# Hybrid decoder block: gate quarters over 110 expert tiles, first block ranked in the queries, picks in halves

## The reference, cut to what matters

```python
# x: 1024 tokens x 1024; mixers (retention, short convolution) come first
def peer_ffn(a, w_q, k1, k2, u, v):                 # a = rms_norm(h)
    q = (af @ w_q).reshape(t, PEER_HEADS, 2, PEER_HALF)              # 8 heads, 2 x 128
    s1 = jnp.einsum('thd,hnd->thn', q[:, :, 0], k1)                  # 128 keys a side
    s2 = jnp.einsum('thd,hnd->thn', q[:, :, 1], k2)
    v1, i1 = lax.top_k(s1, PEER_TOPK); v2, i2 = lax.top_k(s2, PEER_TOPK)      # 16
    cand_s = v1[..., :, None] + v2[..., None, :]                     # 16 x 16 per head
    top_s, top_pos = lax.top_k(cand_s, PEER_TOPK)
    gate = jax.nn.softmax(top_s, axis=-1)            # 8 x 16 experts of 16384 per token
    act = jax.nn.gelu(jnp.einsum('td,ted->te', xb, ue))              # ue = u[idx]
    return jnp.einsum('te,ted->td', gb * act, ve)                    # ve = v[idx]
# then per-layer embeddings, gate and a last rms_norm
```

## Time and profile before

| | us |
|---|---|
| median of 3 runs (3942.32 to 3951.86) | 3949.08 |
| the profiled execution | 3940.36 |
| its span, first to last instruction | 3938.3 |
| PE busy, share of the span | 3514.5 (89%) |
| DVE busy | 2827.3 (72%) |
| POOL busy | 2409.5 (61%) |
| ACT busy | 1008.0 (26%) |
| expert stage, 128 tiles | 1548.1 to 2672.4 |
| value stage, 32 groups | 2672.4 to about 3775 |

### The profile page before, as it was taken

One profiled execution on the slowest core, in us unless ns is written; L12 is line 12 of the kernel. 1 busy time (PEld: TensorE's weight loads), 2 busy tenths in 40 slices (PEclk: granted clock), 3 DMA queues, 4 the chain that ended last, 5 costly groups with the idle time before them and its releaser, 6 DMA issues.

```text
span 3938.3 us, 59196 instructions
## 1 busy us (share of the span) xinstructions
PE 3514.5 (89%) x22379; PEld 3412.9 (87%) x22379; DVE 2827.3 (72%) x4151; ACT 1008.0 (26%) x1654; POOL 2409.5 (61%) x1612
## 2 busy tenths in 40 slices
PE   7899888878989889999999999997889989988877
PEld 6799788777989889988989899997888888888765
DVE  5524477866555654999999999635888888878854
ACT  2310221121000121144545455302222222212132
POOL 5488563325678776876766668865555555555522
PEclk9999899888999999999999999998999999999988
DMA  4244421114666767877878777877888888888811
GB/s 143 77 123 123 128 87 56 45 39 146 217 223 235 249 224 265 297 277 273 285 274 307 277 288 277 314 259 247 277 285 287 282 282 284 287 269 283 276 38 59
DMA packets 324293, 852.82 MB, mean 217 GB/s; under 512 B 27552, under 2 KB 125344, under 8 KB 320672
## 3 DMA queue, kind: packets, MB, share of 16 engines
q0 software_dynamic: 110592, 402.70, 28.0%
q1 hardware_dynamic: 72864, 258.15, 21.6%
q10 hardware_dynamic: 140672, 189.82, 13.8%
HBM read 755.67 MB, written 94.90 MB: 216 GB/s over the span
## 4 chain that ended last, share of the span: by engine, by line
PE 37%; DVE 12%; DMA 5%; POOL 3%; issue 3%; ACT 2%; ACTq 1%; DVEq 0%; POOLq 0%; SPq 0%
PE main L630 26%; PE main L869 7%; DVE h L1853 5%; DMA rows<-v_rows,s_idx 5%; DVE scr L1529 4%; PE scr L828 4%; POOL v_lo L595 2%; ACTq L1207 1%; ACT v_hi L1217 1%; DVE rows L1522 1%; DVE res L1864 1%; POOL rows L568 1%; POOL w_lo L541 0%; PE scr L728 0%; DVE hot L1787 0%
## 5 line engine op out<-in xcount | busy, mean ns | idle before, releaser
L541 POOL TENSOR_TENSOR w_lo<-raw,w_hi 128x1024 fp32r<-128x1024 f32 x346 | 873.2, 2524 | 27.9
L539 POOL CAST w_hi<-raw 128x1024 fp32r<-128x1024 f32 x346 | 367.8, 1063 | 677.5 <-issue 428.6
L630 PE MATMUL main<-mix_hi,w_hi 128*128 128x320 f32 (+1 forms) x2816 | 691.1, 320 | 84.1 <-POOL w_lo L541 44.1
L630 PE MATMUL main<-mix_lo,w_hi 128*128 128x320 f32 (+1 forms) x2816 | 677.9, 315 | 0.0
L630 PE MATMUL main<-mix_hi,w_lo 128*128 128x320 f32 (+1 forms) x2816 | 676.9, 315 | 0.0
L1529 DVE SCALAR_TENSOR_TENSOR scr<-rows,s_dot,scr 128x1024 f32<-128x1024 f32 x381 | 489.1, 1284 | 230.8 <-DMA rows<-v_rows,s_idx 219.0
L869 PE MATMUL main<-h_hi,v_hi 128*128 128x320 f32 x2048 | 490.5, 322 | 120.4 <-DVE res L1864 101.8
L630 PEld LDWEIGHTS main<-mix_hi,w_hi 128*128 128x128 f32 x2816 | 480.7, 191 | 91.5 <-issue 61.6
L568 POOL DMA_INDIRECT rows<-u_rows,s_idx x384 | 405.4, 1056 | 238.1 <-DVE s_dot L1522 134.2
L595 POOL TENSOR_TENSOR v_lo<-raw,v_hi 128x1024 fp32r<-128x1024 f32 x128 | 308.0, 2407 | 389.3 <-ACT v_hi L1217 378.1
L630 PE MATMUL main<-a_hi,w_hi 128*128 128x320 f32 (+1 forms) x1728 | 477.4, 331 | 70.3 <-POOL w_lo L541 43.8
(11 more groups left out here) (231 smaller groups left out, 4967.1 us busy)
## 6 DMA issues: line engine op xcount, KB each, us to landing
raw<-stream SPq DMA_DIRECT2D x474, 512.0 KB
act_d<-actb ACTq DMA_DIRECT2D x128, 320.0 KB
gate_d<-gbuf ACTq DMA_DIRECT2D x20, 2048.0 KB
h<-act_d ACTq DMA_DIRECT2D x128, 320.0 KB, 4.9
gate_in<-gate_d ACTq DMA_DIRECT2D x31, 1280.0 KB, 13.4
rows<-u_rows,s_idx POOLq DMA_INDIRECT x384
rows<-v_rows,s_idx POOLq DMA_INDIRECT x384, 5.8
score_d<-stage ACTq DMA_DIRECT2D x16, 320.0 KB
```

What stands on the lines that cost most here:

```text
L539: pool.tensor_copy(w_hi[:, s, :], raw[:, s, :]).then_inc(hi_made, 1)
L541: pool.tensor_tensor(w_lo[:, s, :], raw[:, s, :], w_hi[:, s, :].bitcast(F32), ALU.subtract) \
L630: last = pe.matmul(main[s][:, dst:dst + n], wt[:, s, c * P:(c + 1) * P], rows[:, c, src:src + n], start=(c == 0 and wt is w_hi and rows is ...
```

## The change

`LEAD` becomes 4 and `SPAN` 22, so that five blocks fill tiles 4 to 113. The 16 quarters of a block come behind tiles 1, 2, 3, 4, 6, 7, 8, 10, 11, 12, 14, 15, 16, 18, 19, 20 of its 22 (`QUARTERS`). The ranks of block 0 move into the queries (`rank_first`), on the scores as they lie in `stage`; before it overwrites `stage`, ACT waits until the last head's have been read. Each pick works in two halves of 4 heads (`pick_keys`): the first behind the rank of head 4, in the middle of the block, the second and the softmax (`pick_rest`) at its end. From the last block on `due` gives 3 rows a tile, so that 499 rows in place of 485 are done by the end of the expert stage, and 269 in place of 283 are spread evenly over the 31 groups. `rank` and the sparse ranks are written as generators, with the same order of instructions ahead of the queries.

```diff
-LEAD = 16
-SPAN = 18
+LEAD = 4
+SPAN = 22
+QUARTERS = [1 + q * (SPAN - 1) // 16 for q in range(16)]
...
-    return max(0, 5 * (min(tile, LAST_ROWS) - PICKED_AT) // 2)
+    steady = 2 * S1 + LEAD + SPAN * (ND - 1)
+    tile = min(tile, LAST_ROWS)
+    return max(0, 5 * (min(tile, steady) - PICKED_AT) // 2 + 3 * max(0, tile - steady))
...
+                if s == 0 and not (isinstance(h, int) and h == 0):
+                    act.wait_ge(head_ranked, h)
                 act.copy(stage[:, s, :], scr[1][:, 0:TDN]).then_inc(scr_drained[1], 1)
...
-                    if k == SPAN - 1 and j + 1 < ND:
+                    if k == QUARTERS[15] and j + 1 < ND:
                         softmax(NS + j + 1, sel_v)
                         if j + 2 < ND:
                             load_scores(j + 2)
...
             for tile in range(2 * Q_PAIR, 2 * S1):
                 dve.wait_ge(tile_done, 2 * S1 + tile)
                 dot_until(due(tile - 1))
+                h, odd = divmod(tile - 2 * Q_PAIR - 3, 2)
+                if h >= 0 and not odd:
+                    rank_first(h)
...
+            rank_first(PH - 1)
+            pick_begin(sel_v[:, :, :], gsum)
+            dot_until(due(2 * S1))
+            pick_keys(0)
+            dot_until(due(2 * S1 + 1))
+            pick_keys(1)
+            dot_until(due(2 * S1 + 2))
+            pick_rest(NS)
+            for j in range(ND):
+                if j + 1 < ND:
                     dve.wait_ge(score_in, 16 * j + 16)
                 for h in range(PH):
+                    if h == 0:
+                        dot_until(due(2 * S1 + LEAD + SPAN * j - 1))
+                        unpack(j)
+                    m = 16 * j + 2 * h
+                    for w in range(2):
+                        hots(m, w)
+                    dot_until(due(2 * S1 + tile_of(m) - 1))
+                    if j + 1 < ND:
+                        for _ in rank_dense(j + 1, h):
+                            pass
+                        if h == PH // 2:
+                            pick_keys(0)
+                        if h == PH - 1:
+                            pick_begin(sel_v[:, :, :], gsum)
+                    for w in range(2):
+                        hots(m + 1, w)
+                    dot_until(due(2 * S1 + tile_of(m + 1) - 1))
...
+                if j + 1 < ND:
+                    pick_keys(1)
+                    pick_rest(NS + j + 1)
...
-                    dot(2 if dt == DC - 1 else 1)
+                    dot(share(share(B_DOTS, b, NGRP - 1), dt, DC))
```

More of the change, by code:

```diff
@@ L96, in due, with share @@
 def due(tile):
-    return max(0, 5 * (min(tile, LAST_ROWS) - PICKED_AT) // 2)
+    steady = 2 * S1 + LEAD + SPAN * (ND - 1)
+    tile = min(tile, LAST_ROWS)
+    return max(0, 5 * (min(tile, steady) - PICKED_AT) // 2 + 3 * max(0, tile - steady))
 A_DOTS = due(LAST_ROWS)
+B_DOTS = DOTS - A_DOTS
+def share(total, i, n):
+    return total * (i + 1) // n - total * i // n
 RING = tuple(range(8))
@@ L597, in _ @@
                 if n >= EG:
-                    for _ in range(3 if n % EG == EG - 1 else 2):
-                        if at_row[0] < DOTS:
-                            gather()
+                    for _ in range(share(B_DOTS, n - EG, NE - EG)):
+                        gather()
             while at_row[0] < DOTS:
@@ L851, in _ @@
                         select(j)
-                    elif k <= 16:
-                        quarter(16 * j + k - 1, first=j if k == 1 else None)
+                    elif k in QUARTERS:
+                        quarter(16 * j + QUARTERS.index(k), first=j if k == 1 else None)
             with pe.Fori(0, (NE - LEAD - SPAN * ND) // 2) as i:
@@ L1160, in _ @@
                 act.wait_ge(score_st[s], 16 * PH + 16)
-            load_scores(0)
+            load_scores(1)
             def gelu(e):
@@ L1393, in settled, with rank @@
                 dve.wait_ge(dve_step, steps.n)
-            def rank(src, v, rest, pairs, pairs_left, index, value, between=lambda: None):
+            def rank(src, v, rest, pairs, pairs_left, index, value):
                 settled()
@@ L1399, in rank @@
                     steps.mark(dve.max(v[:, s, 0:8], src[s]))
-                between()
+                yield
                 settled()
@@ L1430, in rank_sparse, with sparse_parts @@
                 dve.wait_ge(sc_in, 2 * h + 2)
[L1431 to L1435, removed]
+                return rank((sc[:, t, 2 * h, :], sc[:, t, 2 * h + 1, :]), s_v16, s_left, s_cand, s_candl,
+                            lambda a, at: s_ix[:, t, h, a * TOPK + at:a * TOPK + at + 8],
+                            lambda at: s_top[:, t, h, at:at + 8])
+            def sparse_parts():
+                for n in range(NS * PH):
+                    yield from rank_sparse(n)
+                    yield
+            parts = sparse_parts()
             def rank_some(n):
                 for _ in range(n):
-                    if ranked[0] < NS * PH:
-                        rank_sparse(ranked[0])
-                        ranked[0] += 1
+                    next(parts, None)
             def pick_begin(values, sums):
@@ L1457, in pick_key @@
             def pick_key(ix, at, same, dst, which, between=lambda: None):
-                same4 = same[:, :, :].rearrange("p (h k) a -> p h k a", h=PH)
+                heads = ix.shape[1]
+                same4 = same[:, :, :].rearrange("p (h k) a -> p h k a", h=heads)
                 settled()
@@ L1468, in pick_key @@
                     same4, same4,
-                    ix[:, :, which * TOPK:(which + 1) * TOPK].unsqueeze(2).to_broadcast([P, PH, TOPK, TOPK]), ALU.mult))
+                    ix[:, :, which * TOPK:(which + 1) * TOPK].unsqueeze(2).to_broadcast([P, heads, TOPK, TOPK]), ALU.mult))
                 between()
@@ L1775, in _, with rank_first @@
             norm_rows(2, 1, 4 * DC, 0, a_lo[1], a_hi[1])
-            rank_some(6)
+            rank_some(48)
             mixers(1, lambda tile: dot_until(due(tile)))
+            def rank_first(h):
+                m = query_scratch(h, 1)
+                dve.wait_ge(scr_drained[1], m.drained("s1"))
+                for part, _ in enumerate(rank((stage[:, 0, 0:P], stage[:, 1, 0:P]), v16, left, cand, candl,
+                                              lambda a, at: sel_ix[:, h, a * TOPK + at:a * TOPK + at + 8],
+                                              lambda at: sel_v[:, h, at:at + 8])):
+                    if part == 2:
+                        settled()
+                        dve.sem_inc(head_ranked, 1)
             for tile in range(2 * Q_PAIR, 2 * S1):
@@ L1801, in rank_dense, with pick_keys, pick_rest @@
             def rank_dense(j, h):
[L1802 to L1812, removed]
+                return rank((scores[:, 2 * h, :], scores[:, 2 * h + 1, :]), v16, left, cand, candl,
+                            lambda a, at: sel_ix[:, h, a * TOPK + at:a * TOPK + at + 8],
+                            lambda at: sel_v[:, h, at:at + 8])
+            def pick_keys(half):
+                hs = slice(PH // 2 * half, PH // 2 * (half + 1))
+                ks = slice(P // 2 * half, P // 2 * (half + 1))
+                pick_places(sel_ix[:, hs, :], [at[:, hs, :] for at in pos])
+                for which in range(2):
+                    pick_key(sel_ix[:, hs, :], [at[:, hs, :] for at in pos], eq[:, ks, :], picked[:, :, ks], which)
+            def pick_rest(n):
+                pick_end(n, sel_v[:, :, :], gsum, picked[:, 2, :])
                 settled()
@@ L1819, in _ @@
             weigh_sparse(0)
-            for j in range(ND + 1):
-                if j < ND:
+            rank_first(PH - 1)
[8 more added lines that the diff above has]
+                if j + 1 < ND:
                     dve.wait_ge(score_in, 16 * j + 16)
                 for h in range(PH):
[L1824 to L1839, removed]
+                    if h == 0:
[15 more added lines that the diff above has]
+                    dot_until(due(2 * S1 + tile_of(m + 1) - 1))
+                if j == 2:
                     weigh_sparse(1)
-                if j < ND:
-                    pick(NS + j)
+                if j + 1 < ND:
+                    pick_keys(1)
+                    pick_rest(NS + j + 1)
             dot(A_DOTS - at_dot[0])
```

29 lines of the change are left out of this document (15 added, 14 removed).

## The result

The changed kernel takes 3986.36 us (median of 4 runs, 3978.29 to 3992.15), the kernel before 3947.32 beside it (4 runs, 3942.32 to 3951.86): ratio 1.0098, 95% interval 1.0075 to 1.012. It is 39 us slower; the forecast was 14 slower, and its range ended at 3983. The two profiled executions are 48 us apart (spans of 3938.3 and 3986.1), because the one before ran 7 us under its median.

A forecast was written before the change was run, and what follows sets the result against it. PE and DVE were taken as both nearly full, PE losing 79 us in the expert stage. Losses 49 + 23 + 14 + 12 = 98 against 79 (+19.1), value stage -5.4: 3949.1 + 13.7 = 3963, range 3920 to 3983.

The forecast's parts named there:

- (a): Middle of a block: the half pick delays quarter 9's `hots`; PE waits 10.5 and loses 1.7 to slow clock, 49 us.
- The dots that are missing meanwhile hurt nobody: Middle of a block: dots DVE doesn't make during the half pick cost nothing, since quarters wait first.
- (b): Block boundary: the score load queues behind `gate_d`, landing 15.5 after it; first quarters late, 7.8 at three boundaries, 23 us.
- my reason for the 33.6 us: Expert stage before the change: PE waits 33.6 us for `w_lo` because POOL's gathers wait for dots, not made during picks.
- rival 2: Boundary: the score load isn't late, or DVE arrives later anyway; 17 us less than the sum, 3946; chance 0.24.
- (c): Start of the expert stage: DVE's eighth rank, dots and pick make PE wait 11.5 at `select`; 14 us in all.
- (d): Small losses: quarter 15, 4 x 1.5; block 0's first quarters, 2.5; last block's dots and five gather buffers, 3; together 12.
- Rival 4: Last block: 3 rows a tile make the weight stream late, 1 us a tile over 16 tiles, 3979; chance 0.07.
- Rival 1: Expert stage: PE alone bounds it, DVE meeting its deadlines; about 50 us lost in place of 79, 3915; chance 0.22.
- The queries: Seven ranks add 38 us to DVE there, but it is busy only 47 of 128, so they cost nothing.
- DVE can't work ahead: Expert stage: `hots` can't be made before the last quarter is read, so what counts is where a long piece stands.
- The value stage: Even rows cost its groups 0; 2 dots in place of 6 before ACT's copy at the end give -5.4.

The follow-up runs named there:

- Experiment 4: The changed kernel with the half pick in the middle of a block moved behind the `hots` of quarter 9: 3954.68 us, ratio 1.0018.
- experiment 1: The changed kernel with PE's loop over the five blocks written out, nothing else: 3964.86 us, ratio 1.0047.
- experiment 3: The changed kernel with PE's block loop written out and DVE's wait for the scores moved ahead of the first rank: 3947.72 us, ratio 1.0001.
- experiment 6: The kernel before the change with only PE's loop over the blocks written out: 3951.38 us, ratio 1.0013.
- experiment 5: The changed kernel with the three edits: PE's block loop written out, score wait ahead of the first rank, half pick behind quarter 9's `hots`: 3921.76 us, ratio 0.9937.
- experiment 2: The changed kernel with DVE's wait for the next scores moved from ahead of `unpack` to ahead of the first rank reading them: 3977.52 us, ratio 1.0079.
- experiment 9: Third half of the `hots` buffer, added to the changed kernel with the three edits, LEAD 6 and 2.5 rows a tile: 3893.73 us, ratio 0.9867.
- experiment 7: The changed kernel with the three edits and LEAD 6 in place of 4: 3916.79 us, ratio 0.9932.
- experiment 12: The kernel before the change with only its value-stage rows spread evenly over the 31 groups: 3942.65 us, ratio 0.9989.

## Why the forecast had the sign right and the size wrong

- **(a), the middle: right.** 12.2 a block were forecast and 11.6 to 12.9 measured, at quarter 9, by the half pick ahead of its `hots`. Experiment 4 gives 32 of the 49 back by the place alone. "The dots that are missing meanwhile hurt nobody" held in the middle. The mechanism is the forecast's.
- **(b), the boundary: here the forecast failed.** The late load is there, and somewhat later than forecast: it lands 17 behind its issue (15.5), and DVE waits for it 23.6 us in three times, where I had some 5 each. But I took the time at which PE would be ready for the select as its tiles' sum, 7.04 each. The step that failed is this floor of PE at a boundary: PE's jump costs 4.2 to 5.0 us and about 2 of slow clock behind it, four times, a term that the sum doesn't have. The boundaries lost 41.7 in place of 23, and the fourth 7.8 where I had nothing. The sum was short by 18.7 there, out of 24. The trace of before had the four stops. One is printed as "issue", 3.9 us, which I passed over; three are printed as `w_lo`, and I took them for it, so that my reason for the 33.6 us (POOL's gathers wait for dots) is wrong for 13.1 of them. Experiments 1, 3 and 6 show that the stop goes with the loop, and that the old pick covered it; the instruction packets show what it is. The Trainium skill, "Runtime: NRT & Kernel Launch", section "Instruction fetch mechanics", says that a taken branch to code outside the window held near the engine must wait for its fetch, and recommends unrolling where possible. The trace agrees: a packet of the instruction queue in each stop, 4.2 to 5.0 us for a body of 22 tiles in the changed kernel, 3.9 to 4.7 for one of 18 in the kernel before; the loops over two tiles in the lead and the tail show no wait for "issue".
- **(b), rival 2** said that timely scores would give 17 back; taken off the boundary alone they gave 9, since PE's jump lay beside them. Term and rival had the same fault.
- **(c), the start:** 18.2 for 16.5. The wait at select was 10.70 (11.5 forecast). Tile 3 lost 5.4 by a late `w_lo`, for which I had 0.7; in experiments 1, 4 and 5 it lost 0.6, in experiment 2 again 5.4, so it varies. That the sums agree so nearly is in part luck.
- **(d):** quarter 15 as forecast. The last block's 3 was too little: the five buffers, which I priced at almost nothing, stall one tile by 6.8. Rival 4 had the place, and named the weight stream in place of the row buffers.
- **Rival 1** (PE alone is the bound) was the better design's forecast, not this one's: with the jumps gone, the places put right and a third half of `hot`, the kernel comes to 3885, beyond its 3915, while the sum of DVE's work is nearly the same.
- **The queries:** right, no new wait of PE. The sentence that "DVE can't work ahead", since `hots` cannot be made before the last quarter is read, was true of this kernel, and worth 17 us (experiment 9), of which 9 show in its expert stage.
- **The value stage:** the end as forecast (5.4; 5.9 measured). Its groups are open. By the profile the stage ended 1102.9 us behind tile 127 before and 1102.7 after, so its groups took back what the end gave. But in the six other profiles with the changed kernel's 269 rows (experiments 1 to 5 and 7) it took 1091.7 to 1105.4, and why experiment 1's was 8 shorter I can't say. The kernel before and experiment 6 have the same value stage, and there it took 1102.9 and 1112.1; so one profile each doesn't tell even 9 us of groups from chance. For the same reason the profile of experiment 12 (1108.5) doesn't show whether its end's 5.9 reach the whole time, and its median only just does.

## What to carry to other kernels

Count the jumps of every engine's loops among its work: price the first instruction behind each with a large body from the trace, also where another wait lies over it, for it stays when that wait goes. A wait's printed cause may be a neighbour that ended at about the same time: check which tile the named instruction belongs to. Where two engines are nearly full, cost a long piece by what waits behind it at its place, and look for the place where the consumer has its longest pause; moving one half pick gave 32 us here, more than the 23 by which the three edits together beat the kernel before. And when two late things meet at one place, try the edits together as well as apart: alone these two showed 18 of the 29 us that they take off the boundaries.

## What I had not expected of the hardware

A jump back over PE's code of 22 tiles costs 4.2 to 5.0 us in the changed kernel and 3.6 to 4.9 in experiments 2 and 4, one over 18 tiles 3.9 to 4.7, while jumps over two tiles don't show. In all 16 of these stops a 16 KB packet of the instruction queue starts 1.0 to 2.4 us after PE's last matmul, and PE starts again 1.6 to 1.8 us behind its end. The 16 DMA engines are fully busy there (share 0.99 to 1.01 in the changed kernel's four), about four fifths of it with what ACT's queue moves; whether the fetch would be shorter without them isn't tested. Behind the changed kernel's four stops PE ran at the lower clock for 2.7 to 5.7 us: matmul pairs of 0.74 in place of 0.46 us, granted clock 0.50.
